# Order of two groups of weight loads on the sync queue: the last four cross attention chunks and the first six loads of the second feed forward

## What is computed

```python
for l in range(DEPTH):                       # DEPTH = 2
    h = layer_norm(ALPHA * h + 0.5 * swiglu(h, ffn1_gate[l], ffn1_up[l], ffn1_down[l]), ...)
    z = h @ w_in[l]                          # then gated convolution, a recurrence, a pooling
    mix = concatenate([y_conv, y_rec, y_pool]) @ w_out[l]
    h = layer_norm(ALPHA * h + mix, ...)
    h = layer_norm(ALPHA * h + cross_attn(h, mem, ca_q[l], ca_k[l], ca_v[l], ca_o[l]), ...)
    h = layer_norm(ALPHA * h + 0.5 * swiglu(h, ffn2_gate[l], ffn2_up[l], ffn2_down[l]), ...)
```

## Time and profile before

| what | us |
|---|---|
| median of three runs | 3275.48 |
| lowest, highest | 3274.97, 3276.44 |
| the profiled execution | 3292.36 |
| its span, first to last instruction | 3290.4 |

### The profile page before, as it was taken

One profiled execution on the slowest core, in us unless ns is written; L12 is line 12 of the kernel. 1 busy time (PEld: TensorE's weight loads), 2 busy tenths in 40 slices (PEclk: granted clock), 3 DMA queues, 4 the chain that ended last, 5 costly groups with the idle time before them and its releaser, 6 DMA issues.

```text
span 3290.4 us, 39696 instructions
## 1 busy us (share of the span) xinstructions
PE 3087.1 (94%) x13217; PEld 2186.7 (66%) x13217; DVE 2113.9 (64%) x4285; ACT 953.9 (29%) x2505; POOL 1218.6 (37%) x1129
## 2 busy tenths in 40 slices
PE   8999999999999999999999999978999999987777
PEld 5698888887887888887886755533435855542224
DVE  6786788665555456765455596567565587587544
ACT  2310012121001002221002464334446464444333
POOL 1003554343444443353440144444444044444332
PEclk9999999999999999999999999999999999999999
DMA  9688988788998996788996899999999899999998
GB/s 351 232 282 311 382 336 305 269 338 302 352 349 341 360 348 228 241 328 308 372 354 244 321 419 420 420 419 391 405 421 421 300 417 420 419 421 422 421 421 355
DMA packets 252613, 1165.52 MB, mean 354 GB/s; under 512 B 27320, under 2 KB 34968, under 8 KB 186416
## 3 DMA queue, kind: packets, MB, share of 16 engines
q0 software_dynamic: 152784, 825.30, 62.3%
q1 hardware_dynamic: 99632, 338.30, 28.4%
q10 hardware_dynamic: 48, 0.05, 0.0%
HBM read 1162.44 MB, written 1.10 MB: 354 GB/s over the span
## 4 chain that ended last, share of the span: by engine, by line
PE 67%; DMA 18%; DVE 7%; ACT 5%; issue 2%; another core or an unknown queue 1%; POOL 0%; SPq 0%; ACTq 0%; DVEq 0%; POOLq 0%
PE ps_b L1511 17%; PE ps_a L1449 12%; DMA ring<-in_peer_uv,idx 11%; PE ps_a L1519 9%; PE ps_b L780 7%; PE ps_a L767 5%; DMA arena<-in_peer_uv,idx 4%; ACT arena L1740 3%; DVE ring L2925 2%; PE ps_b L789 2%; PE ps_b L1277 2%; DMA ring<-in_ffn 1%; PE ps_b L1270 1%; PE ps_b L1215 1%; ACT L1740 1%
## 5 line engine op out<-in xcount | busy, mean ns | idle before, releaser
L1449 PE MATMUL ps_a<-ring,arena 128*128 128x512 f32 x1728 | 820.9, 610 | 131.1 <-ACT arena L1740 130.4
L742 POOL DMA_INDIRECT ring<-in_peer_uv,idx x448 | 499.8, 1116 | 880.8 <-PE ps_a L1449 623.2
L2925 DVE SCALAR_TENSOR_TENSOR ring<-ring,h_tm 128x1024 f32<-128x1024 f32 x448 | 546.6, 1223 | 385.1 <-DMA ring<-in_peer_uv,idx 379.9
L701 POOL DMA_INDIRECT ring<-in_peer_uv,idx_now x512 | 574.4, 1122 | 421.6 <-DVE arena L2743 159.7
L1449 PEld LDWEIGHTS ps_a<-ring,arena 128*128 128x128 f32 x1728 | 309.4, 191 | 563.4 <-ACT arena L1740 288.1
L1511 PE MATMUL ps_b<-x_t,ring 128*128 128x256 f32 x2816 | 623.6, 380 | 3.5 <-DMA ring<-in_ffn 2.3
L1511 PEld LDWEIGHTS ps_b<-x_t,ring 128*128 128x128 f32 x2816 | 532.4, 190 | 83.8 <-DMA ring<-in_ffn 4.6
L1740 ACT ACTIVATE arena<-ps_b 128x256 f32<-128x256 f32 (+3 forms) x224 | 102.6, 460 | 1252.9 <-PE ps_b L1511 791.0
L1519 PE MATMUL ps_a<-arena,ring 128*128 128x256 f32 x1408 | 318.7, 379 | 0.0
L2743 DVE SCALAR_TENSOR_TENSOR arena<-ring,h_tm 128x1024 f32<-128x1024 f32 x256 | 299.4, 1221 | 22.0 <-DMA ring<-in_peer_uv,idx_now 17.8
L1519 PEld LDWEIGHTS ps_a<-arena,ring 128*128 128x128 f32 x1408 | 267.2, 190 | 39.6 <-issue 3.5
(11 more groups left out here) (448 smaller groups left out, 3349.0 us busy)
## 6 DMA issues: line engine op xcount, KB each, us to landing
ring<-in_ffn SPq DMA_DIRECT2D x264, 512.0 KB
wring<-in_second_w SPq DMA_DIRECT2D x174, 512.0 KB
wring<-in_mix_w SPq DMA_DIRECT2D x128, 512.0 KB
ring<-in_ada_rows POOLq DMA_DIRECT2D x36, 512.0 KB, 6.4
ring<-in_second_w SPq DMA_DIRECT2D x12, 1024.0 KB
ring<-in_peer_uv,idx_now POOLq DMA_INDIRECT x512
ring<-in_peer_uv,idx POOLq DMA_INDIRECT x448
arena<-in_second_w SPq DMA_DIRECT2D x13, 512.0 KB
```

The costliest lines, as they stand in the source:

```text
L701: G.indirect_dma_start(rows[:, s, :], None, table, bass.IndirectOffsetOnAxis(ap=idx_now[:, half, s:s + 1], axis=0)).then_inc(rows_in[s], p ...
L742: G.indirect_dma_start(pairs[slot].rearrange("p c d -> p (c d)"), None, a["peer_uv"], bass.IndirectOffsetOnAxis(ap=idx[:, b, s:s + 1], axi ...
L1449: ins = mm(ps_a[:, b * D + j * 512:b * D + (j + 1) * 512], diags[:, at % DIAGS, :], pairs[at % PAIRS][:, 1, j * 512:(j + 1) * 512], start= ...
L2925: V.scalar_tensor_tensor(row, row, 1.0, h_tm[:, n // SLOTS, :], ALU.mult, ALU.mult, accum_out=dots[:, n % SLOTS:n % SLOTS + 1]).then_inc(d ...
```

## The change

For w = 1 the four chunk loads are issued ahead of the six feed forward loads in place of behind them. Nothing else moves: the modulation rows' chunks stay behind both.

```diff
             for l in range(L):
                 mix_at, row_at = l * MIX_CHUNKS, CTX_MOD_ROWS + 4 * l
                 for w in range(2):
+                    if w:
+                        chunk_loads(a["mix_w"], mix_at + (MIX_CHUNKS - WR), WR)
                     for ft in range(2):
                         for part in range(3):
                             ff_loads(l * (2 * FT) + (w * FT + ft), ft, part)
                     if w == 0:
                         mod_row_loads(row_at)
                     else:
-                        chunk_loads(a["mix_w"], mix_at + (MIX_CHUNKS - WR), WR)
                         mod_row_loads(row_at + 1)
                         mod_row_loads(row_at + 2)
```

## The result

| | us |
|---|---|
| before, median of 7 runs (lowest, highest) | 3275.90 (3273.62, 3281.47) |
| changed, median of 7 runs (lowest, highest) | 3289.88 (3287.40, 3296.48) |
| ratio changed to before, 95% interval | 1.0048 (1.0039 to 1.0057) |
| changed, the profiled execution and its span | 3293.31, 3291.4 |

The change costs 14 us by the medians and 0.48%, 15.7 us, by the ratio. The forecast was 3277.9 us with a range up to 3286; the measured time lies above it, on the side of the slower rival, which had 3285.5.

What follows compares the result with a forecast made beforehand. It took TensorE's chain of products as the bound, with no transfer late. A loss of 2.2 us less a gain of 1.0 gave +1.2 us per layer, +2.4 us on 3275.48: 3277.9 us, range 3270 to 3286.

Steps and rivals of the forecast that it cites:

- the slower rival: At the modulation products: chunk 3.1 us late plus 1.9 us clock fall in each layer, 3285.5 us; chance 0.26.
- What bounds the kernel before: From the cross attention's outputs to the modulation row: TensorE's products; neither the last four chunks nor six loads late.
- The place and the mechanism: First modulation chunk, behind the six loads: x us late delays the mean and whole norm by x.
- The feed forward's own loads: At the feed forward's start: needed 25.9 us after their new issue, hidden with 14 us to spare.
- The queue's own working: From chunk 63's issue to the modulation chunk's landing: 3.3 us plus seven transfers' 9.45 us, 12.75 us.
- The gathers in flight under the shifted clock: Behind chunk 63, TensorE 6.5 us earlier: 1.6 MB of gathers left add 4.1 us; modulation chunk 3.1 us late per layer.
- So they are done, with 0.8 MB or 2 us to spare: In the profiled execution's time, gathers end before the six loads leave: 10.5 MB to move, under 11.30 MB moved before.
- Which clock the timed runs follow: At the attention outputs: timed runs either have the profiled waits or pass 6.5 us earlier; left open, both weighed.
- The unnamed waits: At the attention outputs: ScalarE waits 2.74 and 5.10 us in layer 1 for nothing named; TensorE waits in layer 0.
- The gain taken off: At chunk 60: late by up to 2.1 us in the old order; half, 1.0 us, taken as saved per layer.
- The fall of the clock: TensorE's clock falls to the 1.2 GHz level behind the late chunk's wait: 1.9 us per fall, counted in the slower rival.
- The rival of the stalls: At the attention outputs: six loads cause the unnamed waits; ending them returns 6.5 us per layer, 3262.5 us; chance 0.13.

Runs made afterwards that it cites:

- e2: Changed kernel, but the first modulation row's four chunks issued ahead of the six feed forward loads, against the kernel before: 3275.14 us, ratio 0.9999.
- e1: The change in layer 0 alone, old order in layer 1, against the kernel before: 3283.97 us, ratio 1.0017.
- e5: Changed kernel with VectorE's last 8 of 16 sums, and the 8 gathers waiting on them, behind the layer norm, against the kernel before: 3277.89 us, ratio 1.0011.
- e7: Old order plus 12 products of constants that nobody reads ahead of the modulation products, against the kernel before: 3285.36 us, ratio 1.0030.
- e10: Old order plus 20 products of constants ahead of the modulation products, against the kernel before: 3292.54 us, ratio 1.0052.
- e4: Changed kernel plus 12 products of constants that nobody reads ahead of the modulation products, against the kernel before: 3290.32 us, ratio 1.0045.
- e3: Three of the six feed forward loads ahead of chunks 60 to 63, three behind, against the kernel before: 3288.94 us, ratio 1.0039.
- e8: Changed kernel, but one modulation chunk issued ahead of the six loads, three behind, against the kernel before: 3282.37 us, ratio 1.0021.

## Why the prediction was wrong, point by point

**What bounds the kernel before** was right. No chunk of the old order was waited for in its timed runs to a cost that shows: taking the six loads away from ahead of chunks 60 to 63 (e2) changed nothing clear of 3 us.

**The place and the mechanism** were right. The prediction named the first modulation chunk as where the time is decided, with x us of lateness costing x us; the wait stands on that line in both layers, e1 shows it layer by layer, and e2 ends it. The feed forward's own loads were hidden, as reckoned.

**The queue's own working** was right: 12.75 us reckoned, 13.0 measured in e5.

**The gathers in flight under the shifted clock** is the first step that failed. The prediction let the stretch from 703 us to chunk 63's issue go on at 390 GB/s, as before, and so had 1.6 MB and 4.1 us left; the trace has 8.03 MB at 349 GB/s and 2.47 MB and 6.0 us left. With it the lateness of layer 0 is 5.0 us and not 3.1. The rate was taken over from a stretch with 3.15 MB more to do. Without them the gathers came forward by 1.43 MB and no further. The passage has the condition that GpSimd issues the gathers as soon as VectorE frees the places, and this one didn't hold: GpSimd needs 1.25 us for each and issued its last at 725.68, 0.6 us ahead of chunk 63, so that gathers had to be in flight behind it. Of the 3.1 the prediction then took 2.2, "nearer its full size", where both clocks stood open. e5 shows the term from the other side: without these gathers the new order costs no more than the old.

**"So they are done, with 0.8 MB or 2 us to spare"** rests on the same 390 GB/s. The changed kernel moved 10.49 MB in 703 to 732 us, at 362 GB/s, which is just the 10.5 MB that the passage asks for, so by this rate next to nothing was to spare. No run has the unshifted clock with the new order, so whether it would have cost anything there isn't shown.

**Which clock the timed runs follow.** The prediction left this open and let it pull the forecast towards nothing. The unnamed waits of the trace of before are in none of the other eleven traces, the old order's among them, and e1, e7 and e10 had profiled times like their timed ones (3283.46, 3285.44 and 3295.54 us against medians of 3283.97, 3285.36 and 3292.54), where the trace of before stood 16.9 us above its median. So, as far as the traces go, these waits belong to that one execution, and the shifted reckoning was the one to follow. What made them isn't known.

**The gain taken off**, 1.0 us a layer for chunk 60, was too much. One 0.6 us wait was seen in the old order, and e2 shows no gain clear of its interval.

**The fall of the clock** is the second step that failed: the forecast's sum has a wait of 2.2 us but no fall of the clock behind it; only the rival counts that. In the trace it cost 3.0 and 2.7 us and not the rival's 1.9, since the row's products and the mean ran at the low level. Trace and forecast side by side for one layer: wait 5.3 and tail 2.9 against 2.2 less 1.0. Both layers together are 16.3 us in the trace; the ratio's interval is 12.8 to 18.7 us. How much of the timed runs' loss the clock makes stays open (e4 and e7). The rival had this mechanism, with a chance of 0.26, and its threshold (0.4 MB still to be moved) was passed sixfold. Its 3285.5 us was the nearest of the stated times, yet short by 4.4, as both of its terms were too small.

**The rival of the stalls** fell with e1, whose layer 1 has the six loads at their old place and no stall. Its sign, that the waits vanish in the new trace, was met all the same, and the time went the other way.

## What to carry to other kernels

A load moved later in a queue is put ahead of something: here a chunk needed 13.8 us after chunk 63's issue came behind six loads that had 25.9 us. Look for the first transfer behind the new place, and count from the issue of the last one before it to that one's need. Add to the queue's own time the bytes that other queues still have to move then. For these don't take over the old rate of the stretch that is relieved: here gathers filled 1.43 of the 2.24 MB that came free, at the pace at which GpSimd issued them, and the rest stayed empty. Where a profiled execution is longer than the timed runs by as much as some wait that it can't name, reckon by a timeline without that wait.

## What the hardware showed beyond that

In the traces a wait of 5 us on TensorE cost up to 8: the granted clock went to 0.50 for 6.8 us in layer 0 of the changed kernel, and for 3.4 us in layer 0 of e3 behind a wait of 4.0 us. Behind the 2.5 us of e8's layer 0 it stayed at 1.00. And early issue of half of a group was worth little under full DMA engines: three loads of 0.524 MB taken from ahead of a chunk brought it only 1.1 to 1.2 us forward, where by 1.35 us each they take 4 us, because 1 MB of gathers came in their stead.
